# Whole or half weight instructions in the two opening chunks of each expert

## The reference

```python
N_EXPERTS = 8; TOP_K = 2; D_FF_EXPERT = 3584

def swiglu_2(x, wg, wu, wd):
    return (jax.nn.silu(x @ wg) * (x @ wu)) @ wd

def moe_swiglu(x, router, wg, wu, wd):
    t = x.reshape(bsz * s, d)                       # 256 x 1024
    top_v, top_i = lax.top_k((t @ router).astype(jnp.float32), TOP_K)
    top_w = jax.nn.softmax(top_v, axis=-1)
    gate = jnp.sum(jax.nn.one_hot(top_i, N_EXPERTS) * top_w[..., None], axis=1)
    y = jnp.zeros((bsz * s, d), jnp.float32)
    for e in range(N_EXPERTS):
        y = y + gate[:, e:e + 1] * swiglu_2(t, wg[e], wu[e], wd[e])
    return y
```

## Time and profile before

| What | us |
|---|---|
| median of 3 runs (2859.82 to 2865.1) | 2863.86 |
| the profiled execution's own time | 2867.21 |
| its span, first to last instruction | 2865.4 |
| busy in the span: PE | 2743.8 |
| busy: PEld | 2200.4 |
| busy: DVE | 963.2 |
| busy: ACT | 345.1 |

### The profile page before, as it was taken

The page is one execution under the profiler, slowest core; times in us unless marked ns, Lnnn a source line. Parts: engine busy times, 40 slices in busy tenths (PEclk is TensorE's granted clock), DMA queues, the critical chain, the costliest instruction groups (busy, mean ns, idle before and its releaser), DMA issues.

```text
span 2865.4 us, 80015 instructions
## 1 busy us (share of the span) xinstructions
PE 2743.8 (96%) x37718; PEld 2200.4 (77%) x37718; DVE 963.2 (34%) x1660; ACT 345.1 (12%) x717; POOL 18.5 (1%) x28
## 2 busy tenths in 40 slices
PE   8999998999899999999999999989999999999997
PEld 5777776687677766787657876559998998989996
DVE  2454444445555424544355443450000000000001
ACT  1210022100100012000240001510000000000000
POOL 1000000000000000000000000000000000000000
PEclk9999999999999999999999999999999999999998
DMA  7334413554534432454334543349999999999995
GB/s 196 133 132 161 147 59 119 184 177 155 175 103 167 160 129 97 161 177 143 116 108 148 177 155 135 107 174 382 380 394 364 397 376 371 398 360 380 385 379 201
DMA packets 307908, 620.41 MB, mean 217 GB/s; under 512 B 8886, under 2 KB 126908, under 8 KB 293212
## 3 DMA queue, kind: packets, MB, share of 16 engines
q1 hardware_dynamic: 304688, 606.13, 58.4%
q0 software_dynamic: 2400, 10.09, 1.2%
q10 hardware_dynamic: 588, 0.63, 0.1%
HBM read 615.77 MB, written 1.05 MB: 215 GB/s over the span
## 4 chain that ended last, share of the span: by engine, by line
PE 91%; DVE 4%; DMA 2%; issue 2%; ACT 1%; SPq 0%; DVEq 0%
PE ps L1187 19%; PE ps L1795 19%; PE ps L1115 13%; PE ps L1028 13%; PE ps L1811 9%; PE ps L1039 7%; PE ps L1294 2%; PE ps L1710 2%; DMA arena<-in_moe_w_up 1%; PE ps L1770 1%; PE ps L1743 1%; DMA ring<-in_fox_w_in 1%; PE ps L1498 1%; PE ps L1399 0%; PE ps L1508 0%
## 5 line engine op out<-in xcount | busy, mean ns | idle before, releaser
L1795 PE MATMUL ps<-arena,ring 128*64 128x88 f32 x10752 | 437.9, 239 | 15.9 <-issue 13.2
L1795 PEld LDWEIGHTS ps<-arena,ring 128*64 128x64 f32 x10752 | 422.3, 138 | 26.3 <-issue 22.9
L1115 PE MATMUL ps<-ring,arena 128*128 128x512 f32 x880 | 390.3, 597 | 0.0
L1028 PE MATMUL ps<-xT,ring 128*128 128x256 f32 (+2 forms) x1664 | 369.0, 381 | 2.9 <-DVE xT L1912 1.0
L1028 PEld LDWEIGHTS ps<-xT,ring 128*128 128x128 f32 (+2 forms) x1664 | 312.1, 189 | 59.4 <-issue 12.1
L2624 DVE TENSOR_TENSOR arena<-arena,ps 128x176 f32<-128x176 f32 x112 | 37.8, 338 | 827.4 <-ACT arena L899 827.4
L1115 PEld LDWEIGHTS ps<-ring,arena 128*128 128x128 f32 x880 | 163.2, 190 | 193.2 <-issue 193.1
L1811 PE MATMUL ps<-arena,ring 128*64 128x88 f32 x5376 | 226.4, 239 | 11.3 <-issue 11.2
L1811 PEld LDWEIGHTS ps<-arena,ring 128*64 128x64 f32 x5376 | 215.3, 137 | 14.5 <-issue 14.4
L1187 PEld LDWEIGHTS ps<-xT,ring 128*64 128x64 f32 x2816 | 157.2, 140 | 37.2 <-issue 37.2
L1187 PE MATMUL ps<-xT,ring 128*64 128x128 f32 x2816 | 167.6, 278 | 7.7 <-DVE xT L1912 5.2
(11 more groups left out here) (445 smaller groups left out, 2399.7 us busy)
## 6 DMA issues: line engine op xcount, KB each, us to landing
ring<-in_moe_w_gate SPq DMA_DIRECT2D x56, 2048.0 KB, 10.3
ring<-in_ffn_w_gate_up SPq DMA_DIRECT2D x88, 1024.0 KB, 7.7
ring<-in_moe_w_down SPq DMA_DIRECT2D x84, 1024.0 KB, 14.6
ring<-in_moe_w_up SPq DMA_DIRECT2D x28, 2048.0 KB, 15.2
arena<-in_moe_w_up SPq DMA_DIRECT2D x28, 2048.0 KB, 14.9
ring<-in_ffn_w_down SPq DMA_DIRECT2D x55, 1024.0 KB, 11.0
arena<-in_moe_w_down SPq DMA_DIRECT2D x28, 1024.0 KB, 10.3
ring<-in_fox_w_in SPq DMA_DIRECT2D x20, 768.0 KB, 6.1
```

Source lines behind the costliest of these rows:

```text
L1028: ins = pe.matmul(o, lhsT=w[:, k, c0:c0 + m], rhs=rhs[:, k, :], start=(k == 0), stop=(k == kt - 1))
L1115: return pe.matmul(ps[:, 4 + 2 * i + h, :], lhsT=h_par[:, s * S + i * P:s * S + (i + 1) * P], rhs=w[:, s, h * 512:(h + 1) * 512], start=(c ...
L1795: ins = pe.matmul(ps[h, par, c0:c0 + CAP], lhsT=w[:, k, s, h], rhs=xe[:, k, :], start=(k == 0), stop=(k == KD - 1))
```

## The change

Both `gate_up` and `down` get a parameter `cols`, by default `HALVES`. The opening's two `gate_up` and its one `down` are called with `WHOLE`, one slice of all 128 columns: one instruction loads the 128x128 block and writes all 128 PSUM partitions. The loop and `down(last=True)` keep halves.

```diff
+WHOLE = (slice(0, P),)
...
-                    def gate_up(done=None):
+                    def gate_up(done=None, cols=HALVES):
...
-                                    for h in HALVES:
+                                    for h in cols:
                                         ins = pe.matmul(ps[h, par, c0:c0 + CAP], lhsT=w[:, k, s, h], rhs=xe[:, k, :],
                                                         start=(k == 0), stop=(k == KD - 1))
...
-                    def down(last=False):
+                    def down(last=False, cols=HALVES):
...
-                                for h in HALVES:
+                                for h in cols:
                                     ins = pe.matmul(o[h], lhsT=w[:, s, m * P + h.start:m * P + h.stop],
...
-                    gate_up(ex_down_released[last_slot_] if e > 0 else None)
+                    gate_up(ex_down_released[last_slot_] if e > 0 else None, cols=WHOLE)
...
-                    gate_up()
-                    down()
+                    gate_up(cols=WHOLE)
+                    down(cols=WHOLE)
                     if e > 0:
                         scatter(e - 1, y_tk, old_tk)
                     with pe.Fori(0, M_ROUNDS) as i:
```

## The result

The changed kernel takes 2900.49 us (median of 4 runs, 2898.74 to 2906.48), the one before 2862.32 us (4 runs): a ratio of 1.0134 with a 95% interval of 1.0121 to 1.0148. It is slower by 38.2 us. The forecast was 2902 us. The profiled execution took 2900.14 us with a span of 2898.3 us, 32.9 us more than the one before, which lay 3 to 5 us above its median at a mean granted clock of 0.984 (this one had 0.990). All times here are medians, from which one execution of 6305.63 us (the kernel with only `down` whole) and one of 3230.64 us (the first with exchanged strides), far outside the others, are left out.

The account below looks back on a forecast made before the run. PE's stream was taken as the bound, with whole records bound by their weight load. Terms 45.7 - 6 - 1.6 = +38.1 us on the median 2863.9 gave 2902 us, 1.3% slower; range 2883 to 2915.

Parts of the forecast that it names:

- The bound: Experts' stage: PE's stream sets the time, DMA engines follow; PE waits only 1.7 us for weights.
- The first term, +45.7 us: Openings of eight experts: 2560 half records, 97.0 us, become 1280 whole records at 111.5 ns, 142.7 us, bound by the load.
- The load hides: Rival, openings: the stream covers the whole load, records keep 75.8 ns, only -7.6 us remains: 2856 us; chance 0.04.
- does not overlap at all: Rival, whole records: load and matmul add to 188 ns a record, +143 us: 3000 us; chance 0.02.
- Issue waits, -6 us: Second term: slower openings lose their waits for code, together 5.9 us; the loop's first-pass waits stay.
- Changes of shape, -1.6 us: Third term: two fewer changes between half and whole instructions per expert, 16 in all; between 0 and -3 us.
- The clock: Rival, whole chunks: granted clock falls to half, 0.225 us a record, +191 us: 3053 us; chance 0.02.

Follow-up runs that it names:

- the first with exchanged strides: Changed kernel, but the opening's gate_up takes its 128 weight columns side by side and down every second one; 2896.15 us, at a granted clock of 0.85.
- the written-out loop: Kernel before, with PE's hardware loop written out as twelve chunks of straight code, same matmuls, all halves; 2958.72 us, ratio 1.0333.
- the lighter weight traffic: Kernel before, with only the first four of eight row blocks of each expert's gate and up weights fetched; 2830.66 against 2865.94 us, ratio 0.9879.

## Why the prediction was right

- **The bound.** PE's chain, hardly a wait for weights: right. The slower records went into the time, and the stage's DMA share fell instead of its waits growing.
- **The first term, +45.7 us: right in mechanism, mis-sized.** 1280 records at 111.5 ns were forecast. Measured are 1024 at 117.8 and 256 at 111.7: 149.2 us against 97.0 before, +52.2 us. The 112 ns came from rows whose stationary columns lie side by side. `gate_up`'s do not, and that costs 6 ns a record, 6.3 us in all. The diff had shown the stride (`"p k (n s) -> p k s n"`), and the text did not weigh it. In halves the load is hidden, so the stride cost nothing before: 62 records of `gate_up` and 62 of `down` both take 2.58 us.
- **The load hides / does not overlap at all:** both refuted. 118 and 112 ns stand above the 76 of the stream and below 188; with 66 columns they do not move, with halves a pair of loads takes 60 ns.
- **Issue waits, -6 us: too small.** They fell by 9.5 us, 32.9 to 23.4. The 5.9 us of the openings are gone as said; the rest, 3.6 us, fell mostly in the loop's first pass, which was forecast to stay. With only `gate_up` whole all 27.2 us of issue waits lie outside the openings, against 27.0 before the change, so an effect of the slower opening on the loop is not shown. By the distances of starts above 200 ns between half records the fall is 13.2 us (45.7 to 32.5), since a distance also holds the part of a wait that a record's duration covers, and the DMA waits. That these are waits for code behind the weights is shown by the written-out loop and by the lighter weight traffic.
- **Changes of shape, -1.6 us: right in sign, too large.** What such places take beyond the pace of the records around them, the new one included, went from 2.7 to 1.8 us, -0.9 us. Two of the three changes are gone, behind the transposes and into the scatter. The one into the clearing matmuls was forecast to go too, but a whole record before them still takes 214 ns instead of 118.
- **Sum.** In the profile the stage's PE stream, from the first gather to the last scatter, grew by 34.8 us (936.82 to 971.65). The terms make +52.2 - 13.2 - 0.9 = +38.1. Of the other -3.3 us, 2.3 lie in the scatter of the last expert, which stands outside the change: in the kernel before the clock fell to 0.50 in it, in the changed kernel it did not. That is likely chance, and no part of what the change costs.

```profile
2845.12 6.48 PE L1770 MATMUL ps<-arena 88*128 88x512 f32 x8 [1.20 <-ACT arena L893]
2846.20:2850.50 4.30, 4.30 (x6) 1.66 (x5) 3.33 (x5) 1.28 (x1) 0.00 (x0) 0.50 0.04 10
...
2879.59 3.67 PE L1771 MATMUL ps<-arena 88*128 88x512 f32 x8 [1.20 <-ACT arena L894]
```

- **Luck.** That +38.1 met the medians' +38.2 to 0.1 us is luck: the first term was 6.5 us too small and the second 3.5 to 7 us too small the other way.
- **The clock.** Rightly given little chance at 88 columns (it stayed 1.00 through 1200 us of whole instructions), but on thin ground: L1386's 7.5 us. At 44 columns the same code fell to half clock in every expert. The price of this rival, +191 us, counted the whole records alone; where the clock did fall, it stayed low for 5 to 12 us behind them as well.

## What to carry to other kernels

Compare the time that a matmul streams with the time that its stationary operand takes to load. Float32 weights of 128 columns cost 112 ns here (118 with a stride of two). The scatter's records, with 512 moving columns, stand 429 ns apart, which is two passes at 2.4 GHz; by that pace 134 columns would stream for 112 ns. So, as an estimate, the load is the bound below some 130 moving columns. The runs show it at 8, 44, 65, 66 and 88 columns; in the trace of the kernel before, matmuls of 96 rows by 128 weight columns (L1696) stand 112 ns apart against 128 moving columns, where stream and load are about even, and 216 ns against 256. Below that point two 64-column halves on different PSUM partitions, which load side by side, are faster though they are twice the instructions. When an edit changes what is the bound, ask again what each layout costs: a stride that was hidden may become the price. Straight code at a fast pace has a price too; where the DMA engines are full, count waits for code as a term of their own.

## What the runs showed of the hardware

- A whole float32 load is paced at 112 ns with neighbouring columns and 118 ns with every second column; half loads at 58 to 60 ns a pair, with 32, 44 and 64 moving columns.
- At half granted clock a whole record goes from 118 or 112 ns to 213 ns: the load follows TensorE's clock too, and the difference by the stride is gone.
- Streaming 44 instead of 88 columns in the openings made the changed kernel 131 us slower (3032 against 2900 us) and the kernel before 7 us slower; in both the profile shows half granted clock in and behind these stretches. With 66 columns that happened in one opening of eight, with 88 in none.
- PE's code arrives in 16 KB blocks, one for some 128 half records, and PE goes on 1.2 to 1.6 us after a late one has ended. With the DMA engines full a late block costs up to 2.0 us with 88 columns and 2.5 us with 44; at two thirds of the weight traffic the kernel is 35 us shorter with the same matmuls.
